# Attention's product with V with the operands swapped: probabilities stationary, rows scaled in the copy out, head pairs transposed afterwards

## The reference, cut to what matters

```python
def attend(q, k, v):
    s = jnp.einsum('bqkgd,bskd->bkgqs', q, k).astype(jnp.float32) * (HEAD_DIM ** -0.5)
    p = jax.nn.softmax(s, axis=-1).astype(v.dtype)
    return jnp.einsum('bkgqs,bskd->bqkgd', p, v)
...
mix_x = jnp.concatenate([attn_x, lru_x], axis=-1) @ w_out[l]
...
act = jax.nn.gelu(jnp.einsum('nhkd,nd->nhk', u[idx], xc))
return jnp.einsum('nhk,nhkd->nd', g * act, v[idx])
```

## Time and profile before

| | |
|---|---|
| median of 3 runs | 3096.01 us (3094.7 to 3098.4) |
| the profiled execution | 3099.57 us, its span 3097.7 us |
| TensorE busy | 2520.1 us (81%), 9190 matmuls |
| VectorE busy | 2142.4 us (69%) |
| ScalarE busy | 819.6 us (26%) |
| POOL busy | 2102.9 us (68%) |
| DMA | 1163.76 MB, mean 376 GB/s |
| mean granted clock of TensorE | 0.90 |

### The profile page before, as it was taken

How to read it: one execution, slowest core, us unless ns; L and a number is a source line. 1 busy time by engine, 2 the same in 40 slices (tenths; PEclk the granted TensorE clock), 3 DMA queues, 4 the chain that set the end, 5 groups by cost and what they waited for, 6 DMA issues and landing times.

```text
span 3097.7 us, 29161 instructions
## 1 busy us (share of the span) xinstructions
PE 2520.1 (81%) x9190; PEld 1107.2 (36%) x9190; DVE 2142.4 (69%) x4677; ACT 819.6 (26%) x1848; POOL 2102.9 (68%) x2167
## 2 busy tenths in 40 slices
PE   6978998697788878897789878988888788733598
PEld 4844466333333333323232433233333333211122
DVE  4787587977777776778767877867777777566400
ACT  2358222123212321232223321322123212100122
POOL 5930044667777777777777777777777777777775
PEclk9988999798989998999899888989898989876799
DMA  9532278999999999999999999999999999999998
GB/s 343 177 149 83 92 282 297 407 372 407 415 419 419 419 419 416 419 409 415 418 420 400 419 419 419 416 414 418 411 419 408 419 407 418 419 420 420 411 419 353
DMA packets 335937, 1163.76 MB, mean 376 GB/s; under 512 B 40485, under 2 KB 51365, under 8 KB 333608
## 3 DMA queue, kind: packets, MB, share of 16 engines
q0 software_dynamic: 297792, 1084.36, 86.6%
q1 hardware_dynamic: 37994, 77.54, 7.1%
HBM read 1148.13 MB, written 13.63 MB: 375 GB/s over the span
## 4 chain that ended last, share of the span: by engine, by line
PE 31%; DMA 26%; POOL 18%; DVE 13%; issue 7%; ACT 3%; SPq 1%; DVEq 0%; POOLq 0%; ACTq 0%
POOL arena L608 18%; PE psum L2041 15%; DMA arena<-in_u,idx_u 15%; DMA arena<-in_v,arena 11%; DVE arena L1536 7%; PE psum L1974 3%; PE psum L1752 2%; PE psum L1930 2%; PE psum L1908 1%; PE psum L1903 1%; PE psum L1862 1%; PE psum L1689 1%; PE psum L1915 1%; PE psum L1890 1%; PE psum L1849 1%
## 5 line engine op out<-in xcount | busy, mean ns | idle before, releaser
L2041 PE MATMUL psum<-arena 128*32 128x512 f32 x4096 | 1312.2, 668 | 303.1 <-DMA arena<-in_v,arena 291.9
L1536 DVE CUSTOM_DVE_ANT_0 arena<-arena,psum 128x1024 f32<-128x1024 f32 x1024 | 1230.4, 1219 | 441.7 <-DMA arena<-in_u,idx_u 427.9
L608 POOL DMA_INDIRECT arena<-in_u,idx_u x1024 | 973.5, 951 | 460.5 <-issue 224.6
L608 POOL DMA_INDIRECT arena<-in_v,arena x1024 | 980.3, 957 | 338.8 <-issue 258.5
L2041 PEld LDWEIGHTS psum<-arena 128*32 128x32 f32 x4096 | 378.2, 118 | 1173.5 <-issue 1033.6
L937 ACT ACTIVATE arena<-arena 128x32 f32<-128x32 f32 x1024 | 308.3, 318 | 1234.1 <-PE psum L2041 1232.7
L1974 PE MATMUL psum<-wbig,arena 128*128 128x512 f32 x512 | 230.7, 605 | 1.1 <-ACT arena L899 1.1
L1862 PE MATMUL psum<-kT,arena 64*128 64x512 f32 (+1 forms) x384 | 171.5, 584 | 32.2 <-ACT arena L814 24.6
L1890 PE MATMUL psum<-arena,v 128*64 128x128 f32 x1120 | 147.3, 291 | 26.5 <-ACT arena L861 26.5
L1881 PE MATMUL psum<-ident,arena 128*128 128x128 f32 x560 | 102.9, 300 | 59.3 <-ACT arena L861 44.0
L1890 PEld LDWEIGHTS psum<-arena,v 128*64 128x64 f32 x1120 | 133.8, 147 | 40.2 <-ACT arena L861 40.2
(11 more groups left out here) (265 smaller groups left out, 2180.9 us busy)
## 6 DMA issues: line engine op xcount, KB each, us to landing
arena<-in_u,idx_u POOLq DMA_INDIRECT x1024, 8.6
arena<-in_v,arena POOLq DMA_INDIRECT x1024, 8.8
arena<-in_w_mod POOLq DMA_DIRECT2D x20, 512.0 KB, 5.2
wbig<-in_wq SPq DMA_DIRECT2D x1, 7168.0 KB, 19.8
arena<-in_w_mod SPq DMA_DIRECT2D x12, 512.0 KB, 5.0
arena<-in_xin SPq DMA_DIRECT2D x5, 1024.0 KB, 9.1
arena<-in_w_mod SPq DMA_DIRECT2D x2, 2048.0 KB, 10.6
wbig<-in_w_mod SPq DMA_DIRECT2D x2, 2048.0 KB, 20.5
```

The lines of the kernel that those rows point to most:

```text
L608: pool.indirect_dma_start(ring[:, r, :], None, t[table], bass.IndirectOffsetOnAxis(idx[:, j:j + 1], 0)).then_inc(got[r], 16)
L1536: V.tensor_tensor_reduce(ring[:, r, :], ring[:, r, :], hx_cur, 1.0, 0.0, ALU.mult, ALU.add, act_[:, j:j + 1]).then_inc(S["u_used"], 1)
L2041: ins = M(bank(4 + b)[QP * q:QP * q + QP, :], lhsT=sel[:, j % SELS, :], rhs=ring[:, r, 512 * b:512 * b + 512], start=(i == 0), stop=(i == ...
```

## The change

The product with V takes the transposed probabilities as its stationary operand (128 keys x 128 queries) and 64 columns of `v` as the moving one, so its result is 128 queries x 64 features. The probabilities are no longer scaled: VectorE only inverts the sum (`invert_sum`, semaphore `sum_inverted`), and ScalarE multiplies by it, one value per query, in the copy of the result to `tok` (`move_tok`, semaphore `tok_ready`). `tok` lies over `top` and holds two heads. Each pair is then transposed by TensorE (`turn_pair`) and copied into `att` by ScalarE (`move_pair`), which raises `att_ready` once per pair in place of once per head. Pairs 0, 1 and 2 are turned behind the last group of transposes of heads 2, 4 and 6; pair 3 in `post`, where the order of the output product now takes the tile of pair 3 last. TensorE waits for `probs_ready` in place of `probs_normed`. Chunk 0 has the same with banks 6 and 7.

```diff
+        tok = top
...
         def first_pv(h):
-            return bank(6 + h % 2)[0:64, 2 * P:3 * P]
+            return bank(6 + h % 2)[:, 2 * P:2 * P + HD]
+        def pair_at(n, i):
+            if n == 0:
+                return bank(7 if i == 3 else 6)[:, 3 * P:4 * P]
+            return bank(3)[:, 2 * P:3 * P]
...
+            def move_tok(n, h, pv):
+                o, b = HD * (h % 2), 46 + h % 2
+                act.wait_ge(S["sum_inverted"], n * NQ + h + 1)
+                A(tok[:, o:o + HD], pv, ACT.Copy, scale=small[:, b:b + 1]).then_inc(S["tok_ready"], 1)
+            def move_pair(n, i):
+                if i == 3:
+                    act.wait_ge(S["pair_turned"], n + 1)
+                A(att[:, i, :], pair_at(n, i), ACT.Copy).then_inc(S["att_ready"], 1)
...
                         act.wait_ge(S["pt_ready"], n * ATT_T + l + 1)
+                        if g == 2 and h % 2 == 0 and h:
+                            move_pair(n, h // 2 - 1)
                         A(pT[:, 4 * g:4 * g + k, :], bank(3)[:, 0:k * P], ACT.Copy).then_inc(S["pt_out"], 1)
...
                     act.wait_ge(S["pv_ready"], n * NQ + h + 1)
-                    o = 64 * (h % 2)
-                    A(att[o:o + 64, h // 2, :], bank(3)[0:64, 0:P], ACT.Copy).then_inc(S["att_ready"], 1)
+                    move_tok(n, h, bank(3)[:, 0:HD])
...
             def post(n, cols):
+                if n:
+                    move_pair(n, 3)
...
-            def normalise(n, h):
+            def invert_sum(n, h):
                 b = 46 + h % 2
                 dve.wait_ge(S["probs_ready"], n * NQ + h + 1)
-                ch.link(V.reciprocal(small[:, b:b + 1], small[:, b:b + 1]))
-                V.tensor_scalar(pr, pr, small[:, b:b + 1], None, ALU.mult).then_inc(S["probs_normed"], 1)
+                V.reciprocal(small[:, b:b + 1], small[:, b:b + 1]).then_inc(S["sum_inverted"], 1)
...
+            def turn_pair(n, i):
+                pe.wait_ge(S["tok_ready"], n * NQ + 2 * i + 2)
+                return T(pair_at(n, i), tok, ident[:, :])
...
-                    pe.wait_ge(S["probs_normed"], n * NQ + h + 1)
-                    pe.wait_ge(S["att_ready"], n * NQ + h)
+                    pe.wait_ge(S["probs_ready"], n * NQ + h + 1)
+                    pe.wait_ge(S["tok_ready"], n * NQ + h)
+                    if h:
+                        wait(pe, "att_ready", 4 * n + (h - 1) // 2)
...
+                        if g == 2 and h % 2 == 0 and h:
+                            ins = turn_pair(n, h // 2 - 1)
                         ins.then_inc(S["pt_ready"], 1)
...
-                    pv = bank(3)[0:64, 0:P]
+                    pv = bank(3)[:, 0:HD]
...
-                        ins = M(pv, lhsT=v[:, kt, 64 * (h % 2):64 * (h % 2) + 64], rhs=pT[:, kt, :],
+                        ins = M(pv, lhsT=pT[:, kt, :], rhs=v[:, kt, 64 * (h % 2):64 * (h % 2) + 64],
...
                 fill(OUT_AT)
-                pe.wait_ge(S["att_ready"], n * NQ + NQ)
                 if n:
+                    turn_pair(n, 3).then_inc(S["pair_turned"], 1)
+                    pe.wait_ge(S["att_ready"], 4 * n + 3)
...
                 if n == 0:
-                    for kt in (2, 7, 3):
-                        out_first(kt)
+                    out_first(2)
+                    turn_pair(0, 3).then_inc(S["pair_turned"], 1)
+                    out_first(7)
+                    out_first(3)
                 else:
                     pe.wait_ge(S["z_done"], n)
                     for i in range(2):
-                        for kt in range(KT):
-                            fill(OUT_AT + 3 * i + kt // 3)
+                        for j, kt in enumerate((0, 1, 2, 4, 5, 6, 7, 3)):
+                            fill(OUT_AT + 3 * i + j // 3)
+                            if kt == 3:
+                                pe.wait_ge(S["att_ready"], 4 * n + 4)
                             ins = out(i, kt)
```

More of the change, by code:

```diff
@@ L991, in move_pT @@
                 act.wait_ge(S["pt_ready"], l + 1)
+                if g == 2 and h % 2 == 0 and h:
+                    move_pair(0, h // 2 - 1)
                 A(pT[:, 4 * g:4 * g + k, :], bank(6 + l % 2)[:, 0:k * P], ACT.Copy).then_inc(S["pt_out"], 1)
             def move_pv(h):
-                o = 64 * (h % 2)
                 act.wait_ge(S["pv_ready"], h + 1)
-                A(att[o:o + 64, h // 2, :], first_pv(h), ACT.Copy).then_inc(S["att_ready"], 1)
+                move_tok(0, h, first_pv(h))
+                if h == NQ - 1:
+                    move_pair(0, 3)
             act.wait_ge(S["krot_ready"], NTOK // 2)
@@ L1387, in attention @@
                     fill(first_norm + every * h)
-                    normalise(n, h)
+                    invert_sum(n, h)
                     if h + 1 < NQ:
@@ L1593, in _ @@
                 a = 2 * f
-                normalise(0, a)
+                invert_sum(0, a)
                 if f + 2 < LF:
@@ L1601, in _ @@
                     lru_in(a + 2)
-                    normalise(0, a + 1)
+                    invert_sum(0, a + 1)
                 else:
@@ L1817, in turn_probs @@
                 if g == 0:
-                    pe.wait_ge(S["probs_normed"], h + 1)
+                    pe.wait_ge(S["probs_ready"], h + 1)
                     if h == 0:
@@ L1821, in turn_probs @@
                 else:
-                    wait(pe, "att_ready", h)
+                    wait(pe, "tok_ready", h)
+                    wait(pe, "att_ready", (h - 1) // 2)
                 wait(pe, "pt_out", l - 1)
@@ L1826, in turn_probs @@
                     ins = T(bank(6 + l % 2)[:, j * P:(j + 1) * P], pr[:, kt * P:(kt + 1) * P], ident[:, :])
+                if g == 2 and h % 2 == 0 and h:
+                    ins = turn_pair(0, h // 2 - 1)
                 ins.then_inc(S["pt_ready"], 1)
+            def turn_pair(n, i):
+                pe.wait_ge(S["tok_ready"], n * NQ + 2 * i + 2)
+                return T(pair_at(n, i), tok, ident[:, :])
             def values(h):
@@ L1844, in out_first @@
                 if kt < 4:
-                    pe.wait_ge(S["att_ready"], 2 * kt + 2)
+                    pe.wait_ge(S["att_ready"], kt + 1)
                 else:
@@ L1930, in out @@
                     return M(bank(i), lhsT=att[:, kt, :] if kt < 4 else lc[:, kt - 4, :],
-                             rhs=wo[:, kt, 512 * i:512 * i + 512], start=(kt == 0), stop=(kt == KT - 1))
+                             rhs=wo[:, kt, 512 * i:512 * i + 512], start=(kt == 0), stop=(kt == 3))
                 if n == 0:
-                    for kt in (2, 7, 3):
-                        out_first(kt)
+                    out_first(2)
+                    turn_pair(0, 3).then_inc(S["pair_turned"], 1)
+                    out_first(7)
+                    out_first(3)
                 else:
```

6 lines of the change are left out of this document (3 added, 3 removed).

## The result

The changed kernel takes **3108.33 us** (3103.49 to 3110.97, six runs) against 3096.02 (3094.0 to 3098.4, six runs) for the one before: ratio 1.0032, interval 1.0022 to 1.0043. It is 12.3 us slower, where 12.5 us less was forecast. The profiled execution, 3103.49 (span 3101.7), is the fastest of its six, 4.8 under the median, and that of before lay 3.6 above its median; so the two spans differ by 4.0 only, and stages have to be compared instead.

The account below looks back on a forecast made before the run. POOL's own gather pace (1.2445 us) was taken to bound the kernel after 650 us, attention chains before. Gathers -11.1 and -1.2, chunk 0 -1.1, chunk 1 +0.9 gave -12.5 on 3096.0: 3083.5, range 3068 to 3098.

Parts of the forecast that it names:

- Change 0: Product with V, operands swapped: each instruction taken at 112 ns, paced by the load of 128 columns, so no gain or loss.
- The rival: Products on the chains of chunks 0 and 1: unhidden loads, and low clock slowing two scores (+4.6); 3103.0, chance 0.15.
- unhidden loads: Products with V on the chain: 128-column loads not overlapped cost +4.2 in chunk 0 and +10.7 in chunk 1.
- the faster rival: Products with V on the chain: moving columns set the pace, so they halve, -14.4, 3069.1; chance 0.10.
- these 11.1 us come off the end: Chunks 2 to 7: gather delays beside 48 scalings vanish, and POOL never catches up, so -11.1 us.
- the 1.2 of chunk 1: Chunk 1, last two scalings at 543 and 556 us: gather delays and stalls removed, between 0 and 2.3, taken as 1.2.
- The absorbed rival: Gather stretch: transfers at 419 GB/s return POOL's 12.3 us as later landings, leaving -0.2, 3095.8; chance 0.20.
- lost to disturbances: After 650 us: 1905 gathers at 1.2445 make 2371 of some 2427 us; about 57 us booked as disturbances of POOL.
- Chunk 0: -1.1 forecast: Chunk 0 chain: scalings -1.8 and -0.2, end of chunk -0.2, pair transposes and longer copies +1.1; together -1.1.
- The pair steps: Pair transposes and copies of heads 2 and 4 on chunk 1's chain: 2 x (0.278 + 0.15) = +0.9; hidden in chunks 2 to 7.
- The copy out: ScalarE's scaled copy of the product's result: 0.32 taken against 0.270, +0.05 a head, nearly all beside TensorE's next scores.
- The slower case: Loads of 128 columns and a lower clock at products on the chains of chunks 0 and 1: 3103.0, chance 0.15.

Follow-up runs that it names:

- wide_moving: Changed kernel with 128 columns of v (both heads' values) moving in the product with V, 64 copied out; 3097.45 us, ratio 1.0001 to the kernel before.
- half_moving: Kernel before with only 64 of the 128 query columns moving through the product with V, stationary 64 kept; 3094.02 us, ratio 0.9983.
- no_scaling: Kernel before without the scaling of the probabilities on VectorE, reciprocal kept; 3097.12 us, against 3097.04 for the kernel before beside it.
- short_rows: Kernel before with gathers of 896 of the 1024 columns of each expert row, same count of gathers; 3083.31 us, ratio 0.9951.
- scaling_back: Changed kernel with the scaling on VectorE again and no scale in the copy out; 3108.08 us, ratio 1.0041 to the kernel before.
- wide_chunks_2_7_again: Changed kernel with 128 moving columns in the products with V of chunks 2 to 7 only, second series; 3106.97 us, ratio 1.0033 to the kernel before.
- wide_chunks_0_1: Changed kernel with 128 moving columns in chunks 0 and 1 only; 3469.22 us on the slow chip (kernel before 3483.93), 3097.67 when run again.
- short_rows_wide: Changed kernel with 896-column gathers and 128 moving columns in all products with V; 3454.11 us in the slow series, 3061.57 when run again.

## Why the prediction was wrong

**The step that failed first: "Change 0" for the product.** Its own duration came out as costed: 2.44 for 20 at the high clock (the 2.4 expected), 4.53 all at the low level for 4.0 to 4.1 partly at it. Its loads take 192 ns as in the earlier trace rows, and its median matmul 275, the same as in wide_moving with 128 moving columns. What the step left out is what comes behind. It took the rise of the clock behind a product for given, though no row had a product with 64 moving columns ahead of that rise. The rival had the right fork ("if it does not rise behind the new product") and a wrong price: it costed two scores, +4.6; in the runs two scores did go slow, and the transposes, the projections and parts of the products as well, 11.6 in all. The other half of that rival, unhidden loads at +4.2 and +10.7, did not come: wide_moving has the same loads and none of the loss.

The Trainium skill ("TensorE: Matmul & The Clock Gate", section "LDWEIGHTS (loading the stationary operand)") has a load's time go by its stationary columns; the loads of the products agree (137 ns for 64, 192 for 128, 333 for 128 at the low level), while a transpose's load of 128 columns takes 140. The table in its section "Back-to-back issue gap" goes by moving columns alone; by it the product would halve. That section gives the table for a single matmul and says that in a stream of loads and matmuls both set the spacing, which the prediction passed over. The traces agree: beside the short load of half_moving the product nearly halved (69 ns for 117), beside the load of 128 it did not (122). So the faster rival falls, on the load it had against it.

**The second: "these 11.1 us come off the end".** They did not, nor the 1.2 of chunk 1. The absorbed rival was right: no_scaling 3097.12 against 3097.04. The argument used against it, that gathers go on at the same 1.2445 after a delay, was a local reading: over the loop as a whole a delay taken away comes back in POOL's gaps of over 0.4 us (41.0 to 55.4 us). The sign was in the trace of before. Of the 57 us that the prediction booked as "lost to disturbances", 11.1 are the delays and 41.0 are these gaps, at which POOL waited for a buffer; a queue that nothing holds has none, as short_rows shows. 1.2445 us a gather of 0.5 MB is 421 GB/s, and the slices stand at 419: POOL's pace and the transfers' rate coincide within half a per cent. So the removed delays gave nothing while rows were whole, and an eighth fewer bytes took only 5.0 off the loop while the delays stayed. The delays themselves were sized about right: 11.1 forecast, 10 to 16 once rows are short.

**Chunk 0: -1.1 forecast**, by two scalings on the chain. From the first scores of chunk 0 to the squares of the norm behind it the profile has 1.6 less (137.2 for 138.8), but scaling_back, with the scaling, has 1.3 of it, and no_scaling, without it, is 0.4 longer. The chain named one of two branches of nearly equal length. Whether the change gained anything here stays open: wide_chunks_2_7_again has the chunk 0 of the kernel after and takes 138.4, short_rows has that of the kernel before and takes 136.4, so single profiles scatter by more than the term. The opening moves the first gather too, with no edit near it (by 3.8).

**The pair steps, +0.9 in chunk 1**, fit in the sum: with the clock restored chunk 1 is 0.9 longer than before (258.4 for 257.5), 1.2 with short rows. The steps themselves are smaller. In wide_moving the transpose adds 0.12 and the copy, though it lasts 0.28, holds the next one up by 0.17 only, so two pairs make 0.6; that the whole comes to 0.9 is partly luck. The copy out takes 0.314 for the 0.32 taken.

**Chances.** Two rivals came true together, absorbed (-0.2 left) and the low clock in chunk 1 (+11.6): 3096 - 0.2 + 11.6 = 3107, against 3108.3 measured. The prediction priced each alone, the clock on top of a gain that wasn't there, and so its range ended at 3098. The slower case that it priced (3103) lay outside that range, as it said itself. None of the versions with the whole computation beats the kernel before: the best, wide_moving and wide_chunks_0_1, are level with it.

## What to carry to other kernels

Before halving the moving columns of a product on the critical path, look at the granted clock around it and ask what is to raise it afterwards; what follows the product may cost more than the product can save. A delay on an issuing queue counts only if what it feeds has room: compare the bytes of one issue over its pace with the rate in the slices, and look on the queue's timeline for gaps longer than its usual one. If the two rates agree within a per cent and there are such gaps, price the delay at nothing until one of them is moved. Where a chain alternates between engines of near-equal load, a step on it is worth only its lead over the other branch.

## What the runs showed of the hardware

- With 64 moving columns in the products the granted clock is lower for what comes behind, with a stationary operand of 64 (mean 0.92 to 0.89 in the loop) as of 128 (0.92 to 0.88); in chunk 1 with 128 stationary a low stretch that began in a product reached from 472 to past 486 us. Twice the columns at the same loads took 10.6 us off.
- A scaling of 1280 columns from SBUF to SBUF on VectorE delays a gather's issue beside it, by 0.23 us in the mean; a row maximum of the same tile, longer by 0.6, stretches none of the gathers beside its 48 instances. The Trainium skill ("SBUF — State Buffer", section "Who interferes with whom") has the one block the other for the whole instruction where VectorE is in a mode that uses the shared port pair. The trace agrees that the kind of operation decides; a block for the whole 0.9 was in none of the 48, the most was 0.70.
- On one chip every kernel took 12% more time, with transfers at 362 to 365 GB/s for 416 from 700 to 2700 us. Slower transfers alone don't explain it: with an eighth fewer bytes (short_rows_wide, 321 GB/s) the time was hardly shorter, 3454.11 for 3459.85. In wide_chunks_0_1 POOL waited 203 us there for releasers that the profile can't name, which no other series shows. The cause is open.
